# A two-layer hybrid encoder step: the heads' sums of squares as two rounded products each, and shorter norm fillers

## The chip, the cores and the metric

One Trainium2 chip, one of its cores. The metric is the device time in microseconds (us) of one execution of the whole program; lower is better.

## The reference, cut to what matters

T = 320 tokens (256 of a prompt, 64 of a running stream) of 1024 features go through two layers. Each layer is a mixer (a combined input projection, a short convolution beside a gated linear attention of 4 heads, an output projection), a layer norm, a feed-forward block (dense in layer 0, top 2 of 8 experts in layer 1) and a second layer norm. All data is float32. The change lies in the norm of the heads' outputs:

```python
o, new_s = _gla_chunked(qh, kh, vh, ah, gla_s)          # o: (B, T, 4 heads, 128)
o = o * lax.rsqrt(jnp.mean(jnp.square(o), axis=-1, keepdims=True) + LN_EPS) * gla_norm_g
y_gla = o.reshape(B, T, GLA_DV) * jax.nn.silu(g)
out = jnp.concatenate([y_conv, y_gla], axis=-1) @ w_out
```

## The kernel before, in words

Features lie on the 128 partitions and the 320 tokens along the free dimension, so a head's output is one tile of 128x320 and the sum over a head's 128 values is a sum over partitions. TensorE does it: a product with a 128x128 matrix of ones puts the sum on every partition.

Large products are made from rounded operands. A weight unit (1 MB, 128x2048) is loaded into `raw` (a ring of 6), ScalarE rounds it into `whi` (ring of 3, L1144), VectorE writes the rest into `wlo` (L1462), and TensorE adds three products of fast rounded operands (hi*hi, hi*lo, lo*hi; L664 to L666). An ordinary float32 product takes TensorE more passes; the trace shows it as two matmul records. The ones product L841 is of that kind.

All engines' programs are written out by hand, in order, with semaphores between them; there is no planner. In a mixer, TensorE works through 12 units of the input projection (24 rounded products for each of two output tiles, 48 in all) and 4 units of the output projection. On each engine `hooks` says what stands behind unit u. What matters here, per layer:

- Behind unit 8, TensorE computes the heads' outputs (`outputs`). VectorE copies them to `og` (`read_o`, L1656) and then does half of the convolution (`conv_tiles(0)`, L1700 to L1709). ScalarE squares them (`squares`, L1261) into `proj`.
- VectorE's unit 9: the rest of unit 11 (L1462), then `conv_tiles(1)`. VectorE's unit 10: the rest of unit 12 (the first of the output projection, L1462), then `weigh_o` (L1664, L1668), `rest_y` (L1731), `conv_out(0)` (L1720), `rest_y`. Its unit 11: `conv_out(1)` (L1720, waits until ScalarE has copied out the last projection tile), `rest_y`, the rest of unit 13 (L1462), and then the rest of unit 14 and the first residual tile.
- Behind unit 9 TensorE does the sums of squares (`mean_squares`, L841), then goes on with units 10 and 11. ScalarE turns the sums into 1/rms (`rms`) and afterwards rounds unit 12.
- ScalarE's unit 10 ends in rounding six of the eight tiles of y (L1282), each behind VectorE; its unit 11 copies the last two projection tiles (L1299), rounds unit 13 (L1144), and rounds the last two tiles of y.
- Output projection: TensorE waits for each rest tile of y in its first unit, and for the rest of unit 13 at its second. VectorE adds each product to the residual (L1761), ScalarE squares that (L1181) and only then rounds the next unit, whose rest VectorE takes next.
- `norm` (L725 on): the sums for the layer norm, then up to the next block TensorE has 7 filler matmuls (L744) behind norm 0 (after mixer 0) and norm 1 (after the dense block), none behind norm 2. The first product of the next block waits for `xl`, which VectorE writes (L1551).

The tile `y_split` lies in the memory of `proj`: its tiles 0 to 3 and 4 to 7 are free of other data at this point. `kg` (two tiles) is last read by the scores, before `outputs`.

Of the kernel before, what the change touches and what calls it, by code (L numbers as in the profile page):

```python
# [17 lines left out]
F32 = mybir.dt.float32  # L18
F32R = mybir.dt.float32r
I32 = mybir.dt.int32  # L20
ALU = mybir.AluOpType
ACT = mybir.ActivationFunctionType
AXX = mybir.AxisListType.X

P = 128
# [8 lines left out]
def hybrid_stream_step(nc, x_prompt, x_sample, cache_conv, state_gla, ln_mix_g, ln_mix_b, w_in, w_alpha2,  # L34
# [5 lines left out]
    T = SEQ + DEC  # L40
    _, _, HEADS, DK, DV = state_gla.shape
# [3 lines left out]
    E = moe_router.shape[2]  # L45
# [4 lines left out]
    TT = -(-T // P)  # L50
# [19 lines left out]
    TQ, TK, TV, TG = 0, 2, 4, 8  # L70
# [51 lines left out]
    with ctx:  # L122
        def sb(name, shape, dt=F32):
            return ctx.enter_context(nc.sbuf_tensor(name, shape, dt))

        def sem(name):
            return ctx.enter_context(nc.semaphore(name))
# [5 lines left out]
        x = sb("x", [P, KT, T])  # L133
        ident = sb("ident", [P, P])
        mean_d = sb("mean_d", [P, P])
        ones = sb("ones", [P, P])
        before = sb("before", [P, P])
        slot_no = sb("slot_no", [P, P])
        lower_e = sb("lower_e", [P, E, E])
# [6 lines left out]
        w_split = sb("w_split", [P, DEPTH * KT * LRC + P - LRC], F32R)  # L146
# [30 lines left out]
        def sbm(name, shape, dt=F32):  # L177
            return mix.enter_context(nc.sbuf_tensor(name, shape, dt))

        proj = sbm("proj", [P, 24, T])  # L180
# [3 lines left out]
        og = sbm("og", [P, HEADS, T])  # L184
        gb = og[:, 0:PAIRS, :]
        gc = og[:, PAIRS:2 * PAIRS, :]
        kg = sbm("kg", [P, PAIRS, T])
# [19 lines left out]
        y_split = over_proj.enter_context(nc.sbuf_tensor("y_split", [P, 16, T], F32R))  # L207
# [19 lines left out]
        def sbx(stack, name, shape, dt=F32):  # L227
# [79 lines left out]
        ps = [ctx.enter_context(nc.psum_tensor(f"ps{b}", [P, 512], F32)) for b in range(8)]  # L307
# [21 lines left out]
        by_layer = lambda name: [sem(f"{name}{l}") for l in range(DEPTH)]  # L329
# [1 line left out]
            "proj_ready", "lr_done", "lr_ready", "z_done", "gate_act", "gate_dve"))  # L331
        kd_turned, v_turned, kd_read, v_read, score_done, score_read = (by_layer(n) for n in (
            "kd_turned", "v_turned", "kd_read", "v_read", "score_done", "score_read"))
        ds_done, st_step, o_done, o_read, o_sq, ms_done, ms_act, og_step = (by_layer(n) for n in (
            "ds_done", "st_step", "o_done", "o_read", "o_sq", "ms_done", "ms_act", "og_step"))
        silu_done, cv_step, y_conv, rows_ready, rows_turned, rowsT_ready, yh_ready, yl_ready, r_ready = (
            by_layer(n) for n in ("silu_done", "cv_step", "y_conv", "rows_ready", "rows_turned", "rowsT_ready",
                                  "yh_ready", "yl_ready", "r_ready"))
# [48 lines left out]
        BUSY = {"x lands": 5, "x tile": 2, "first unit": 1, "norm": 4, "router norm": 15, "logits": 3, "first gather": 5}  # L387
# [135 lines left out]
        def _(pool):  # L523
            done = 0

            def const(ins):

                nonlocal done
                done += 1
                ins.then_inc(const_step, 1)  # L530
                pool.wait_ge(const_step, done)
# [3 lines left out]
                                     pattern=[[-1, P]], channel_multiplier=1))  # L535
            const(pool.memset(mean_d[:], 1.0 / D))
            const(pool.memset(w_wide[:, KT * E:], 0.0))
            const(pool.memset(ones[:], 1.0))
            const(pool.memset(cst[:, 0:1], LN_EPS))
            const(pool.memset(cst[:, 1:2], 1.0))  # L540
            const(pool.memset(keep[:], 1.0))
            const(pool.memset(keep[:].rearrange("p (c t) -> p c t", t=CHUNK)[:, :, 0:1], 0.0))

            const(pool.affine_select(out=before[:], in_=ones[:], compare_op=ALU.is_gt, fill=0.0, base=0,
                                     pattern=[[1, P]], channel_multiplier=-1))
            const(pool.memset(lower_e[:], 1.0))
            const(pool.affine_select(out=lower_e[:], in_=lower_e[:], compare_op=ALU.is_gt, fill=0.0, base=0,
# [28 lines left out]
            for l in range(DEPTH):  # L576

                pool.wait_ge(rowsT_ready[l], 1)
                n = (CONV_W - 1) * CT
# [7 lines left out]
                if l == 0:  # L587
# [6 lines left out]
                    fill = STATIC * P  # L594
# [65 lines left out]
        def _(pe):  # L660
# [32 lines left out]
            def keep_busy(n, bank=ps[7]):  # L693

                for _ in range(n):
                    pe.matmul(bank[:, 0:P], mean_d[:], mean_d[:], start=True, stop=True)
# [4 lines left out]
            def turn_x(k, t):  # L701
                return pe.transpose(ps[X_BANK[k]][:, P * t:P * t + TOK[t]], x_in[0:TOK[t], t, P * k:P * k + P],
                                    ident[0:TOK[t], 0:TOK[t]])

            for h in range(2):
                for t in range(TT):
                    keep_busy(BUSY["x tile"], ps[1])
                    pe.wait_ge(x_landed[h][t], 16)
                    for k in range(KT // 2 * h, min(KT // 2 * h + KT // 2, X_EARLY)):
                        mm = turn_x(k, t)  # L710
                        if t == TT - 1:
                            mm.then_inc(x_turned, 1)
            for k in range(X_EARLY, KT):
                pe.wait_ge(x_ready, k - X_EARLY + 1)
                for t in range(TT):
                    mm = turn_x(k, t)
# [8 lines left out]
            def norm(stage, wait_last):  # L725

                idle = ps[0 if stage == 3 else 7]
                pe.wait_ge(summed, (KT - 1) * (stage + 1))
                pe.matmul(ps[4][:, 0:T], mean_d[:], rstd[:], start=True, stop=False)
                wait_last()  # L730
                pe.matmul(ps[4][:, 0:T], mean_d[:], x[:, KT - 1, :], start=False, stop=True).then_inc(mean_done, 1)
                pe.wait_ge(squared, KT * (stage + 1))
                pe.matmul(ps[5][:, 0:T], mean_d[:], sq[:, (KT - 1) % 3, :], start=True, stop=False)
                pe.wait_ge(sq_summed, (KT - 1) * (stage + 1))
                pe.matmul(ps[5][:, 0:T], mean_d[:], sq_sum, start=False, stop=True).then_inc(msq_done, 1)
                if stage in PE_NORMS:
                    pe.wait_ge(mean_copied, stage + 1)
                    for k in range(OWN, KT):
                        pe.matmul(ps[C_BANK[k]][:, 0:T], ident[:], x[:, k, :], start=True, stop=False)
                        pe.matmul(ps[C_BANK[k]][:, 0:T], ident[:], neg_mean_x, start=False, stop=True  # L740
                                  ).then_inc(turned_in, 1)
                    if stage < 2:
                        for m in (96, P, 64, P, 32, P, 96):
                            pe.matmul(idle[0:m, :], w_split[:, 0:m], w_split[:, 0:512], start=True, stop=True)  # L744

            def mixer(l):
                def gates():
# [90 lines left out]
                def mean_squares():  # L838
                    for h in range(HEADS):
                        pe.wait_ge(o_sq[l], h + 1)  # L840
                        pe.matmul(ps[4 + h][:, 0:T], ones[:], proj[:, h, :], start=True, stop=True  # L841
                                  ).then_inc(ms_done[l], 1)

                hooks = {1: gates, 5: turn_kv, 6: scores, 7: states, 8: outputs, 9: mean_squares}
# [18 lines left out]
                for u in range(1, 12):  # L863
                    n = U_IN[l] + u
# [3 lines left out]
                    for half in range(2):  # L868
# [6 lines left out]
                        mm = split_product(ps[(2 * u + half) % 4][:, 0:T], tiles[KT // 2:], False, True)  # L875
# [6 lines left out]
                for u in range(UNITS_OUT):  # L882
                    n = U_OUT[l] + u
# [4 lines left out]
                    for half in range(2):  # L888
                        m = 2 * u + half
                        if m >= 4:  # L890
                            pe.wait_ge(r_ready[l], m - 3)
                        mm = split_product(ps[m % 4][:, 0:T], by_tile(n, KT, half, y_hi, y_lo), True, True)
# [60 lines left out]
            def router():  # L953
                for k in range(KT):
                    pe.wait_ge(x_ready, 3 * KT + k + 1)
                    mm = pe.matmul(ps[0][:, 0:T], w_wide[:, E * k:E * k + P], x[:, k, :], start=k == 0, stop=k == KT - 1)
                mm.then_inc(lg_done, 1)
                for j in XT_ORDER[:2]:
                    turn_rows(j)

                pe.wait_ge(rt_step, RT_LOGITS)
                for t in range(TT):
                    mm = pe.transpose(ps[1][0:TOK[t], E * t:E * t + E], lgT[:, P * t:P * t + TOK[t]], ident[0:E, 0:E])
                mm.then_inc(lg_turned, 1)
                for j in XT_ORDER[2:]:
                    turn_rows(j)
                keep_busy(BUSY["logits"], ps[0])

                pe.wait_ge(rt_step, RT_SEL)
                sel_by = lambda a, b: sel[:, a:b, :].rearrange("p t e -> p (t e)")  # L970
                pe.matmul(ps[1][:, 0:E * TT], before[:], sel_by(0, TT), start=True, stop=False)
                for t in range(1, TT):
                    pe.matmul(ps[1][:, E * t:E * TT], ones[:], sel_by(0, TT - t), start=False, stop=t == TT - 1)
                for t in range(TT):
                    mm = pe.matmul(ps[1][:, E * TT:E * TT + E], ones[:], sel_by(t, t + 1), start=t == 0, stop=t == TT - 1)
                mm.then_inc(pos_done, 1)

                keep_busy(BUSY["first gather"], ps[0])
                pe.wait_ge(cleared, 5)
                pe.wait_ge(pick_ready, 1)  # L980
                for g in range(GATHERS):
                    pe.wait_ge(xtl_ready, TT if g < 2 else 2 * TT)
                    if g < 2:
                        pe.wait_ge(acc_ready, g + 1)
                    if g >= 2:
                        pe.wait_ge(job_read, g - 1)
                    gather(g, ps[6 + g % 2])
# [149 lines left out]
        def _(act):  # L1137
# [71 lines left out]
            def mixer(l):  # L1209
# [45 lines left out]
                def squares():  # L1255
                    act.preload_act_table_set(LOG_EXP)

                    act.wait_ge(o_done[l], HEADS)
                    for h in range(HEADS):
                        act.wait_ge(o_read[l], h + 1)  # L1260
                        act.activation(proj[:, h, :], og[:, h, :], ACT.Square).then_inc(o_sq[l], 1)  # L1261

                def rms():

# [23 lines left out]
                for u in range(12):  # L1288
                    n = U_IN[l] + u
# [167 lines left out]
        def _(dve):  # L1457
# [116 lines left out]
            def mixer(l):  # L1574
# [78 lines left out]
                def read_o():  # L1653
                    for h in range(HEADS):
                        dve.wait_ge(o_done[l], h + 1)
                        dve.tensor_copy(og[:, h, :], ps[4 + h][:, 0:T]).then_inc(o_read[l], 1)  # L1656

                def weigh_o():

# [90 lines left out]
                for u in range(UNITS_OUT):  # L1750
                    n = U_OUT[l] + u
                    rest_unit(n + AHEAD)
                    for half in range(2):
                        m = 2 * u + half
# [410 lines left out]
```

## Time and profile before

| | us |
|---|---|
| median of 3 runs | 1575.9 |
| lowest, highest | 1575.33, 1576.31 |
| the profiled execution's own time | 1575.52 |
| its span in the trace | 1574.0 |
| TensorE (PE) busy | 1558.3 |
| VectorE (DVE) busy | 1238.9 |
| ScalarE (ACT) busy | 1021.7 |
| GpSimd (POOL) busy | 62.4 |

The span leaves out 1.5 us of the execution's time. A matmul's record covers its way through the array, so records overlap: the distance between two starts is what a product costs, not the length of its record. The granted clock of TensorE was 0.999 of full speed over the span. In timelines the first two columns are the start and the length in us; a bracket at the end is the engine's idle time before the instruction and what ended it.

### The profile page before, as it was taken

How to read it: one execution, taken by the hardware profiler on the slowest of the kernel's cores; microseconds unless marked ns; L12 is line 12 of the kernel's file. 1: busy time of each engine (PE TensorE's matmuls, PEld its weight loads, DVE VectorE, ACT ScalarE, POOL GpSimd, SP SyncE). 2: the span in 40 equal slices, each digit the busy share in tenths (PEclk: the TensorE clock that was granted, in tenths of full speed). 3: DMA queues.
4: the chain of work that ended last, by engine and by line, in shares of the span. 5: the costliest groups of instructions: out<-in, count | busy, mean ns of one | idle time of the engine just before them, and what ended most of it. 6: DMA issues, size and time to landing. Idle time of an engine off the chain costs nothing.

```text
span 1574.0 us, 23366 instructions
## 1 busy us (share of the span) xinstructions
PE 1558.3 (99%) x8489; PEld 1375.7 (87%) x8489; DVE 1238.9 (79%) x1414; ACT 1021.7 (65%) x1182; POOL 62.4 (4%) x97
## 2 busy tenths in 40 slices
PE   9999999999999999999999999999999999999997
PEld 8999999999999998888788888888888888888886
DVE  5577545445475688999899988989998999998996
ACT  4454333333354457778678878778878778777885
POOL 1002100000020010000200000000000001000100
PEclk9999999999999999999999999999999999999999
DMA  9524954444434344999999999999999999999992
GB/s 280 196 81 141 369 192 135 158 136 157 154 114 135 108 141 159 374 369 383 397 395 394 393 376 379 395 390 371 379 373 376 395 392 387 387 395 384 391 393 98
DMA packets 229902, 457.44 MB, mean 291 GB/s; under 512 B 10930, under 2 KB 73088, under 8 KB 229760
## 3 DMA queue, kind: packets, MB, share of 16 engines
q1 hardware_dynamic: 224288, 434.16, 76.2%
q0 software_dynamic: 5520, 22.04, 3.6%
q8 instruction: 57, 0.93, 0.2%
q14 instruction: 37, 0.30, 0.1%
HBM read 441.74 MB, written 17.58 MB: 292 GB/s over the span
## 4 chain that ended last, share of the span: by engine, by line
PE 93%; DVE 3%; DMA 1%; issue 1%; ACT 1%; SPq 0%; DVEq 0%; ACTq 0%
PE ps L1045 18%; PE ps L1020 12%; PE ps L1022 12%; PE ps L1021 12%; PE ps L664 11%; PE ps L665 11%; PE ps L666 11%; DVE wlo L1467 2%; PE ps L1058 1%; DMA raw<-in_moe_w_down 1%; DMA proj<-in_x_prompt 0%; PE ps L1094 0%; PE ps L826 0%; PE ps L1071 0%; PE ps L995 0%
## 5 line engine op out<-in xcount | busy, mean ns | idle before, releaser
L1467 DVE TENSOR_TENSOR wlo<-raw,whi 128x1024 fp32r<-128x1024 f32 x672 | 779.2, 1220 | 47.2 <-ACT whi L1148 45.7
L1148 ACT ACTIVATE whi<-raw 128x1024 fp32r<-128x1024 f32 x672 | 675.6, 1055 | 67.1 <-PE ps L1045 42.8
L1020 PE MATMUL ps<-whi,xg 128*128 128x512 f32 x896 | 354.1, 395 | 1.3 <-DVE wlo L1467 1.3
L1022 PE MATMUL ps<-whi,xg 128*128 128x512 f32 x896 | 349.5, 390 | 0.0
L1021 PE MATMUL ps<-wlo,xg 128*128 128x512 f32 x896 | 349.0, 389 | 0.0
L1462 DVE TENSOR_TENSOR wlo<-raw,whi 128x2048 fp32r<-128x2048 f32 x72 | 165.2, 2295 | 127.7 <-ACT whi L1144 127.7
L664 PE MATMUL ps<-xh,whi 128*128 128x320 f32 x832 | 259.4, 312 | 0.0
L666 PE MATMUL ps<-xh,wlo 128*128 128x320 f32 x832 | 257.1, 309 | 0.0
L665 PE MATMUL ps<-xl,whi 128*128 128x320 f32 x832 | 257.0, 309 | 0.0
L1022 PEld LDWEIGHTS ps<-whi,xg 128*128 128x128 f32 x896 | 168.2, 188 | 35.9
L1020 PEld LDWEIGHTS ps<-whi,xg 128*128 128x128 f32 x896 | 168.3, 188 | 35.3 <-issue 1.4
L1021 PEld LDWEIGHTS ps<-wlo,xg 128*128 128x128 f32 x896 | 168.4, 188 | 33.6
L1144 ACT ACTIVATE whi<-raw 128x2048 fp32r<-128x2048 f32 x72 | 137.3, 1906 | 62.5 <-PE ps L666 56.1
L664 PEld LDWEIGHTS ps<-xh,whi 128*128 128x128 f32 x832 | 156.2, 188 | 3.1 <-issue 1.4
L665 PEld LDWEIGHTS ps<-xl,whi 128*128 128x128 f32 x832 | 156.2, 188 | 0.2
L666 PEld LDWEIGHTS ps<-xh,wlo 128*128 128x128 f32 x832 | 156.2, 188 | 0.0
L1045 PE MATMUL ps<-whi,hT_hi 128*128 128x512 f32 x440 | 136.5, 391 | 0.8 <-DVE wlo L1467 0.8
L1045 PE MATMUL ps<-wlo,hT_hi 128*128 128x512 f32 x440 | 135.6, 389 | 0.0
L1045 PE MATMUL ps<-whi,hT_lo 128*128 128x512 f32 x440 | 135.5, 389 | 0.0
L1045 PEld LDWEIGHTS ps<-whi,hT_lo 128*128 128x128 f32 x440 | 82.6, 188 | 17.4
L1045 PEld LDWEIGHTS ps<-wlo,hT_hi 128*128 128x128 f32 x440 | 82.6, 188 | 17.3
L1045 PEld LDWEIGHTS ps<-whi,hT_hi 128*128 128x128 f32 x440 | 81.8, 188 | 17.5 <-issue 1.1
(351 smaller groups left out, 1420.1 us busy)
## 6 DMA issues: line engine op xcount, KB each, us to landing
raw<-in_moe_w_gate SPq DMA_DIRECT2D x112, 1024.0 KB, 8.5
raw<-in_moe_w_up SPq DMA_DIRECT2D x112, 1024.0 KB, 8.9
raw<-in_moe_w_down SPq DMA_DIRECT2D x112, 1024.0 KB, 7.8
raw<-in_w_in SPq DMA_DIRECT2D x23, 1024.0 KB, 7.5
raw<-in_ffn_w_gate SPq DMA_DIRECT2D x14, 1024.0 KB, 5.0
raw<-in_ffn_w_up SPq DMA_DIRECT2D x14, 1024.0 KB, 5.0
raw<-in_ffn_w_down SPq DMA_DIRECT2D x14, 1024.0 KB, 5.1
raw<-in_w_out SPq DMA_DIRECT2D x8, 1024.0 KB, 5.2
```

Of the source, the lines that this page charges most:

```text
L664: pe.matmul(out, wh, hi, start=start and j == 0, stop=False)
L665: pe.matmul(out, wh, lo, start=False, stop=False)
L666: mm = pe.matmul(out, wl, hi, start=False, stop=stop and j == len(pairs) - 1)
L1020: pe.matmul(bank[:], xh_k, wh, start=k == 0, stop=False)
L1021: pe.matmul(bank[:], xh_k, wl, start=False, stop=False)
L1022: mm = pe.matmul(bank[:], xl_k, wh, start=False, stop=k == KT - 1)
L1045: mm = pe.matmul(ps[4 + d][:], hT[:, c % 2, k, :], slot(w, n, SPLIT, 2)[:, j, 512 * d:512 * d + 512], start=fc == 0 and k == 0 and hT is h ...
L1058: mm = pe.transpose(bank[:, P * f:P * f + P], hm[:, c % 2, P * f:P * f + P], ident[:])
L1144: act.activation(flat(whi, n, SPLIT), flat(raw, n, RAW), ACT.Copy).then_inc(hi_ready, 2)
L1148: act.activation(part(whi, n, SPLIT, h), part(raw, n, RAW, h), ACT.Copy).then_inc(hi_ready, 1)
L1462: dve.tensor_tensor(flat(wlo, n, SPLIT), flat(raw, n, RAW), flat(whi, n, SPLIT).bitcast(F32), ALU.subtract).then_inc(lo_ready, 2)
L1467: dve.tensor_tensor(part(wlo, n, SPLIT, h), part(raw, n, RAW, h), part(whi, n, SPLIT, h).bitcast(F32), ALU.subtract).then_inc(lo_ready, 1)
```

## The change

- The matrix of ones becomes a tile of the rounded type (`ones_r`); its float32 view serves all other uses.
- ScalarE's squares are written rounded, into `y_split` tiles 0 to 3.
- VectorE, directly behind the four copies of `read_o` and ahead of `conv_tiles(0)`, gets 8 operations of 128x320: for each head the square once more, unrounded, into one of the two tiles of `kg`, and the difference from the rounded square into `y_split` tiles 4 to 7.
- TensorE's 4 float32 products (L841) become 8 rounded ones, hi and lo of each head added in PSUM; the second waits for VectorE.
- The 7 fillers behind norms 0 and 1 (rounded operands, 512 columns) become `keep_busy(4)`: 4 float32 products of `mean_d` with 128 columns.

```diff
-        ones = sb("ones", [P, P])
+        ones_r = sb("ones_r", [P, P], F32R)
+        ones = ones_r[:, :].bitcast(F32)
...
-                    if stage < 2:
-                        for m in (96, P, 64, P, 32, P, 96):
-                            pe.matmul(idle[0:m, :], w_split[:, 0:m], w_split[:, 0:512], start=True, stop=True)
+                    keep_busy(BUSY["norm"] if stage < 2 else 0, idle)
...
                         pe.wait_ge(o_sq[l], h + 1)
-                        pe.matmul(ps[4 + h][:, 0:T], ones[:], proj[:, h, :], start=True, stop=True
+                        pe.matmul(ps[4 + h][:, 0:T], ones_r[:], y_split[:, h, :], start=True, stop=False)
+                        pe.wait_ge(o_sq_lo, 2 * (HEADS * l + h) + 2)
+                        pe.matmul(ps[4 + h][:, 0:T], ones_r[:], y_split[:, TV + h, :], start=False, stop=True
                                   ).then_inc(ms_done[l], 1)
...
-                        act.wait_ge(o_read[l], h + 1)
-                        act.activation(proj[:, h, :], og[:, h, :], ACT.Square).then_inc(o_sq[l], 1)
+                        act.wait_ge(o_read, HEADS * l + h + 1)
+                        act.activation(y_split[:, h, :], og[:, h, :], ACT.Square).then_inc(o_sq[l], 1)
...
                         dve.wait_ge(o_done[l], h + 1)
-                        dve.tensor_copy(og[:, h, :], ps[4 + h][:, 0:T]).then_inc(o_read[l], 1)
+                        dve.tensor_copy(og[:, h, :], ps[4 + h][:, 0:T]).then_inc(o_read, 1)
+                    for h in range(HEADS):
+                        dve.wait_ge(o_read, HEADS * l + h + 1)
+                        dve.tensor_tensor(kg[:, h % 2, :], og[:, h, :], og[:, h, :], ALU.mult).then_inc(o_sq_lo, 1)
+                        dve.wait_ge(o_sq[l], h + 1)
+                        dve.wait_ge(o_sq_lo, 2 * (HEADS * l + h) + 1)
+                        dve.tensor_tensor(y_split[:, TV + h, :], kg[:, h % 2, :], y_split[:, h, :].bitcast(F32),
+                                          ALU.subtract).then_inc(o_sq_lo, 1)
```

## Rows read from the trace of the kernel before

**Rows 1.** Page, part 1: busy us, share of the span, instructions of each engine
```profile
PE 1558.3 (99%) x8489; PEld 1375.7 (87%) x8489; DVE 1238.9 (79%) x1414; ACT 1021.7 (65%) x1182; POOL 62.4 (4%) x97
```
**Rows 2.** Page, part 4: the chain that ended last, by engine
```profile
PE 93%; DVE 3%; DMA 1%; issue 1%; ACT 1%; SPq 0%; DVEq 0%; ACTq 0%
```
**Rows 3.** Timeline, layer 0, TensorE around the sums of squares
```profile
97.25 0.31 PE L666 MATMUL ps<-xh,wlo 128*128 128x320 f32 x1
97.40 2.31 PE L841 MATMUL ps<-proj,ones 128*128 128x320 f32 x8
...
99.70 0.31 PE L665 MATMUL ps<-xl,whi 128*128 128x320 f32 x1
```
**Rows 4.** Timeline, layer 0, VectorE from the heads' outputs to unit 13
```profile
91.74 0.42 DVE L1700 TENSOR_TENSOR u_mem<-proj 128x256 f32<-128x256 f32 x1
...
95.89 2.29 DVE L1462 TENSOR_TENSOR wlo<-raw,whi 128x2048 fp32r<-128x2048 f32 x1
...
103.62 2.29 DVE L1462 TENSOR_TENSOR wlo<-raw,whi 128x2048 fp32r<-128x2048 f32 x1 [1.30 <-ACT whi L1144]
105.83 0.55 DVE L1664 SCALAR_TENSOR_TENSOR og<-og,prm,proj 128x320 f32<-128x320 f32 x1
106.41 0.49 DVE L1668 TENSOR_TENSOR og<-og,proj 128x320 f32<-128x320 f32 x1
106.82 0.54 DVE L1664 SCALAR_TENSOR_TENSOR og<-og,prm,proj 128x320 f32<-128x320 f32 x1
...
114.37 0.42 DVE L1720 TENSOR_TENSOR proj<-proj,v_tok 128x256 f32<-128x256 f32 x1 [0.91 <-ACT proj L1299]
...
117.27 2.28 DVE L1462 TENSOR_TENSOR wlo<-raw,whi 128x2048 fp32r<-128x2048 f32 x1
```
**Rows 5.** Timeline, layer 0, ScalarE at the last projection tiles
```profile
112.83 0.42 ACT L1299 ACTIVATE proj<-ps 128x320 f32<-128x320 f32 x1
113.83 0.44 ACT L1299 ACTIVATE proj<-ps 128x320 f32<-128x320 f32 x1 [0.57 <-PE ps L666]
114.16 1.91 ACT L1144 ACTIVATE whi<-raw 128x2048 fp32r<-128x2048 f32 x1
```
**Rows 6.** Timeline, layer 0, TensorE: output units 12, 13, and its last product
```profile
113.63 0.31 PE L664 MATMUL ps<-y_split,whi 128*128 128x320 f32 x1
...
120.67 0.31 PE L664 MATMUL ps<-y_split,whi 128*128 128x320 f32 x1
...
141.64 0.31 PE L666 MATMUL ps<-y_split,wlo 128*128 128x320 f32 x1
```
**Rows 7.** Timeline, layer 0, VectorE: residual tiles 1, 3 and 7 of the output projection
```profile
122.58 0.48 DVE L1761 SCALAR_TENSOR_TENSOR x<-x,ps 128x320 f32<-128x320 f32 x1
...
129.01 0.48 DVE L1761 SCALAR_TENSOR_TENSOR x<-x,ps 128x320 f32<-128x320 f32 x1
...
141.99 0.49 DVE L1761 SCALAR_TENSOR_TENSOR x<-x,ps 128x320 f32<-128x320 f32 x1
```
**Rows 8.** Timeline, layer 1, VectorE: rest of unit 13, residual tiles 5 and 7
```profile
557.06 2.29 DVE L1462 TENSOR_TENSOR wlo<-raw,whi 128x2048 fp32r<-128x2048 f32 x1
...
574.74 0.49 DVE L1761 SCALAR_TENSOR_TENSOR x<-x,ps 128x320 f32<-128x320 f32 x1 [0.28 <-PE ps L666]
...
581.78 0.49 DVE L1761 SCALAR_TENSOR_TENSOR x<-x,ps 128x320 f32<-128x320 f32 x1 [1.38 <-PE ps L666]
```
**Rows 9.** Timeline, layer 1, TensorE: first product of output unit 13
```profile
560.46 0.31 PE L664 MATMUL ps<-y_split,whi 128*128 128x320 f32 x1
```
**Rows 10.** Timeline, norm 0: fillers, first and third rest tile
```profile
147.24 2.03 PE L744 MATMUL ps<-w_split 128*96 128x512 f32 x7
...
148.09 0.55 DVE L1551 SCALAR_TENSOR_TENSOR xl<-x,prm,xh 128x320 fp32r<-128x320 f32 x1
...
151.02 0.19 PEld L664 LDWEIGHTS ps<-xh,whi 128*128 128x128 f32 x1 [0.25 <-DVE xl L1551]
```
**Rows 11.** Windows near the end: length, busy us by engine, granted clock, DMA
```profile
1568.00:1570.00 2.00, 0.00 (x0) 0.00 (x0) 2.00 (x4) 0.50 (x2) 0.00 (x0) 0.93 0.70 262
```

More of the change, by code:

```diff
@@ L333, in hybrid_stream_step @@
             "kd_turned", "v_turned", "kd_read", "v_read", "score_done", "score_read"))
-        ds_done, st_step, o_done, o_read, o_sq, ms_done, ms_act, og_step = (by_layer(n) for n in (
-            "ds_done", "st_step", "o_done", "o_read", "o_sq", "ms_done", "ms_act", "og_step"))
+        ds_done, st_step, o_done, o_sq, ms_done, ms_act, og_step = (by_layer(n) for n in (
+            "ds_done", "st_step", "o_done", "o_sq", "ms_done", "ms_act", "og_step"))
+        o_read, o_sq_lo = sem("o_read"), sem("o_sq_lo")
         silu_done, cv_step, y_conv, rows_ready, rows_turned, rowsT_ready, yh_ready, yl_ready, r_ready = (
@@ L537, in _ @@
             const(pool.memset(w_wide[:, KT * E:], 0.0))
-            const(pool.memset(ones[:], 1.0))
+            const(pool.memset(ones, 1.0))
             const(pool.memset(cst[:, 0:1], LN_EPS))
@@ L542, in _ @@
             const(pool.memset(keep[:].rearrange("p (c t) -> p c t", t=CHUNK)[:, :, 0:1], 0.0))
-            const(pool.affine_select(out=before[:], in_=ones[:], compare_op=ALU.is_gt, fill=0.0, base=0,
+            const(pool.affine_select(out=before[:], in_=ones, compare_op=ALU.is_gt, fill=0.0, base=0,
                                      pattern=[[1, P]], channel_multiplier=-1))
@@ L972, in router @@
                 for t in range(1, TT):
-                    pe.matmul(ps[1][:, E * t:E * TT], ones[:], sel_by(0, TT - t), start=False, stop=t == TT - 1)
+                    pe.matmul(ps[1][:, E * t:E * TT], ones, sel_by(0, TT - t), start=False, stop=t == TT - 1)
                 for t in range(TT):
-                    mm = pe.matmul(ps[1][:, E * TT:E * TT + E], ones[:], sel_by(t, t + 1), start=t == 0, stop=t == TT - 1)
+                    mm = pe.matmul(ps[1][:, E * TT:E * TT + E], ones, sel_by(t, t + 1), start=t == 0, stop=t == TT - 1)
                 mm.then_inc(pos_done, 1)
```

## The prediction

> **What bounds the kernel now.** I read the busy times first: TensorE is busy for 1558.3 of 1574.0 us, VectorE for 79% [rows 1]. The chain that ended last says the same: 93% of it is TensorE, 3% VectorE [rows 2]. So a microsecond taken from TensorE's stream is a microsecond gained, but only where no other engine is next in line. The 3% of VectorE warn of places where it is, so I then read the timelines of the mixer, engine by engine. The reader is to see two clocks there. TensorE's: an output unit of 48 products takes 120.67 - 113.63 = 7.04 us, 0.147 us a product [rows 6]. VectorE's: from one residual tile to its counterpart a unit later it needs 6.43 us (122.58 to 129.01), and two such steps further it would be at 141.87; the row says 141.99 [rows 7], 0.12 us late, because TensorE's last product only started at 141.64 [rows 6]. VectorE enters the output projection late, makes up 0.6 us a unit, and has just caught up when the norm begins. There is nothing left for it to lose there.
>
> **TensorE's part: the gain.** The eight records L841 of a layer occupy the stream from 97.40 to 99.55 (the product at 99.70 is the second behind them, so one distance of 0.147 earlier) [rows 3], 2.15 us. Eight rounded products of 320 columns at 0.147 take 1.17 us. Saved: 0.98 us a layer, 1.96 us in both. That the new ones run at 0.147 is taken from L664 to L666, same shape and type. The new second product of each head waits for VectorE's rest. VectorE is at this point at 91.74 [rows 4], and even with the dearest price below it is done by 96.5, 0.9 us before TensorE arrives at 97.40: that wait costs nothing.
>
> **VectorE's part: the price.** Per layer 4 squares and 4 differences of 128x320 go in at 91.74, ahead of the convolution. The nearest rows are L1664 and L1668 [rows 4]. A tensor-tensor operation lasts 0.49 us; the next one that doesn't depend on it starts 0.41 us after it (106.41 to 106.82); one that waits for its predecessor's result starts 0.03 us after that one's end (105.83 + 0.55 to 106.41). So a head costs 0.49 + 0.03 + 0.41 = 0.93 us and the block 3.72 us. Bounds: 8 x 0.41 = 3.3 us if nothing waited, and 8 x 0.58 = 4.6 us if each operation cost what the dependent pair shows from start to start. I take 3.72, as the code alternates just like L1664 and L1668. The differences wait for ScalarE's squares too, but these are made at the pace of the copies and are ahead.
>
> The Trainium skill, "VectorE: DVE Perf Modes", section "The DRAIN you can't avoid", says that the next operation does not start until the pipe is empty, and that a semaphore costs nothing on top. By that the block would be 8 x 0.49 = 3.9 us and the sum below 0.4 us larger. The rows disagree: 106.82 lies 0.08 us before the end of the operation started at 106.41.
>
> **Where the 3.72 us go.** I follow them down VectorE's program in layer 0.
> - The rest of unit 11 moves from 95.89 to 99.6 and ends at 101.9 [rows 4]. TensorE needs it 7.04 us before 113.63, at 106.6, or 105.6 with its gain [rows 6]. Hidden.
> - Ahead of the rest of unit 12 VectorE had 1.30 us idle, waiting for ScalarE; with the 0.08 by which an operation may start before its predecessor's end 1.38 us are absorbed. Left: 2.34 us.
> - `weigh_o` and everything on y moves by 2.34. ScalarE follows, as it rounds y tile by tile. Its copy of the tile before the last moves from 112.83 to 115.17, the last one follows 0.33 later (113.83 to 114.16 is that distance) at 115.50, where it was at 113.83 and had waited 0.57 for TensorE [rows 5]. Left: 1.67 us.
> - VectorE's own wait there (0.91, at 114.37) gives nothing more, as it waits for that very copy. The rest of unit 13 goes from 117.27 to 118.94 and ends at 121.22 [rows 4].
> - TensorE, 0.98 early, would start unit 13 at 119.69. It gets its rest at 121.22, and 0.10 later starts (114.27 to 114.37 is that distance from one engine's end to another's start [rows 4, 5]): 121.32 in place of 120.67, 0.65 late. The gain is gone here, a new wait stands in its place.
> - It does not end there. VectorE and ScalarE enter the output projection 1.67 us later than before, and their own period of 6.43 us is no shorter. Residual tiles 1 and 3 come at 124.25 and 130.68, tile 7 at 141.87 + 1.67 = 143.54 where it was at 141.99: 1.55 us late. TensorE is only 0.65 late by then, and idles for 0.9 us before the norm's last sum. Everything after this is a chain through the norm. Layer 0: +1.55 us.
>
> Layer 1 has the same program and the same waits, except in its output projection. There VectorE already waits for TensorE before residual tiles 5 and 7, 0.28 and 1.38 us [rows 8], so its lag of 1.67 is swallowed down to what TensorE itself is late. That is again the rest of unit 13: 557.06 + 2.29 + 1.67 + 0.10 = 561.12 against 560.46 [rows 8, 9]. Layer 1: +0.66 us.
>
> **The fillers.** The seven start at 147.24 and end their stream about when the first rest tile is written: it is started at 148.09 and done at 148.64. Four short ones end earlier and may let the first product start up to 0.2 us sooner. That is worth nothing: at the third tile (151.02) TensorE waits for VectorE's `xl` by 0.25 us [rows 10], and goes on doing so, so VectorE's pace sets that stretch. Bounds: a gain of 0.2 us at each of the two places, a loss only through the clock (below). I take 0. The rounded type of the ones matrix and the semaphores cost nothing; the DMA queue SP is moved only in that loads wait for rests up to 3.7 us later, with six units of lead. The expert stage is TensorE's (rows 1 and 2), so what the mixers lose is not made up there.
>
> **Sum.** 1.55 + 0.66 + 0 = +2.2 us on the profiled execution's 1575.52 (span 1574.0, 1.5 around it): 1577.7. The median of the runs shown, 1575.9, is 0.4 above that execution, so I forecast 1578.1, 0.14% slower. A measurement of this kernel can tell about 0.2%, 3.15 us, from no change, so this counts as the same.
>
> **Rivals.**
> - *The block is dearer, and the change is slower by over 0.2%.* Beyond the absorbed parts each microsecond of the block arrives twice, once a layer: total = 2 x block - 5.2. At 4.64 us a block, where each of the 8 operations takes the 0.58 of the dependent pair, it is +4.1 us: 1580.0. It passes +3.15 at a block of 4.2 us. For it: every operation of the block touches what its neighbour or ScalarE has just written, and the differences wait on two semaphores. Against: 0.41 behind L1668, which has waits behind it too.
> - *VectorE's work is hidden, TensorE's gain stands*: -1.96 and up to -0.4 from the fillers: 1573.7. For it: VectorE is idle 21% of the time, with gaps of 1.30 and 0.91 in this very stretch. Against: both gaps end with ScalarE, which itself follows VectorE or TensorE, and only 2.05 us are swallowed.
> - *The lag vanishes before the norm in layer 0 as well* (if ScalarE's rounding, not VectorE, sets the 6.43): then both layers lose 0.66, +1.3: 1577.2. Against: the lag of 1.67 sits in both engines.
> - *The clock falls behind the shorter fillers.* They leave TensorE idle some 0.6 us ahead of the next block. In a stretch of 2 us without any matmul near the end, the granted clock was still 0.93 on the mean, and only then went to half (2.4 to 1.2 GHz) [rows 11]. If it fell, a product of the first unit would take twice 0.147, up to 7 us at each of two places: 1585 or more.
>  The Trainium skill, "TensorE: Matmul & The Clock Gate", section "HAM oscillation — how this bites in real kernels", warns that idle gaps let the gate fall and make the next products cold. That would be this rival's time; the rows 11 don't bear it out for a gap this short.
> - *The change doesn't do what it says*: the rounded ones product might run at the float32 pace, then nothing is saved on TensorE. As VectorE sets both layers' ends, that would change little: unit 13 starts at 121.3 either way.
>
> **Chances.** Forecast 0.52 (0.12 of it beyond +3.15, as an error of 0.5 us in a block would do it), dearer block 0.20, hidden 0.12, lag vanishes early 0.10, clock 0.03, something else 0.03. Over 0.2% faster would need more than the whole saving of TensorE: 0.05. Slower: 0.12 + 0.17 of the dearer block + 0.03 of the clock = 0.32. The same: 0.63. The range takes in the hidden case nearly and the dearer block: 1574.2 to 1580.6. The forecast's own range is 1576.8 to 1579.6.
>
> **What would show it.** Right: TensorE's sums of squares take 1.2 us a layer without a wait; 8 operations in 3.7 us on VectorE; a wait of TensorE for `wlo` of 1 us or more at the second output unit in both mixers, in part already at y's last two rest tiles; residual tile 7 of layer 0 right behind VectorE's own work, with TensorE idle 0.9 us; in layer 1 none there; the wait at the third tile behind the norms unchanged; clock 1.00 throughout. Wrong: no idle time of TensorE ahead of unit 13; a block of over 4.2 us or under 3.3; a granted clock below 1 behind a norm; or a changed expert stage, which nothing here touches.

## The result, and the profile after

The changed kernel takes 1578.8 us (median of 20 runs, 1577.94 to 1580.28) against 1575.64 for the kernel before, measured beside it (20 runs, 1574.93 to 1576.81). The ratio is 1.0018 with a 95% interval of 1.0012 to 1.0025: 2.8 us slower by the ratio (the two medians lie 3.16 apart). That is within the 0.2% that the prediction counts as the same, but the interval leaves out no change at all: it is a small loss. The forecast was 1578.1, or +2.2 us.

The page, parts 1 and 4, of the changed kernel:

```profile
span 1577.3 us, 23394 instructions
...
PE 1557.9 (99%) x8491; PEld 1375.5 (87%) x8491; DVE 1245.6 (79%) x1430; ACT 1020.4 (65%) x1182; POOL 62.6 (4%) x97
...
PE 87%; DVE 7%; issue 2%; ACT 2%; DMA 1%; SPq 0%; DVEq 0%; ACTq 0%
```

TensorE is as busy as before (1557.9 against 1558.3 us [rows 1]), VectorE 6.7 us busier. The chain that ended last says where the time went: TensorE's share fell from 93% to 87%, VectorE's rose from 3% to 7% [rows 2]. The busy times alone would not tell it.

TensorE at the sums of squares, layer 0, where [rows 3] had eight records of 0.27 us distance:

```profile
97.46 0.31 PE L668 MATMUL ps<-xh,wlo 128*128 128x320 f32 x1
97.61 0.31 PE L841 MATMUL ps<-y_split,ones_r 128*128 128x320 f32 x1
97.75 0.31 PE L843 MATMUL ps<-y_split,ones_r 128*128 128x320 f32 x1
...
98.64 0.31 PE L843 MATMUL ps<-y_split,ones_r 128*128 128x320 f32 x1
98.78 0.31 PE L666 MATMUL ps<-xh,whi 128*128 128x320 f32 x1
```

97.61 to 98.78 is 1.17 us for the eight, no wait among them: the gain of 0.98 us a layer is there. (All of this trace lies 0.21 us later than the one before when it comes to the heads' outputs, which is the chance of the start.) VectorE, layer 0, beside [rows 4]:

```profile
91.95 0.48 DVE L1661 TENSOR_TENSOR kg<-og 128x320 f32<-128x320 f32 x1
92.53 0.49 DVE L1664 TENSOR_TENSOR y_split<-kg,y_split 128x320 fp32r<-128x320 f32 x1
92.94 0.48 DVE L1661 TENSOR_TENSOR kg<-og 128x320 f32<-128x320 f32 x1
...
95.94 0.42 DVE L1709 TENSOR_TENSOR u_mem<-proj 128x256 f32<-128x256 f32 x1
...
106.43 2.29 DVE L1464 TENSOR_TENSOR wlo<-raw,whi 128x2048 fp32r<-128x2048 f32 x1
...
116.48 0.43 DVE L1729 TENSOR_TENSOR proj<-proj,v_tok 128x256 f32<-128x256 f32 x1 [0.23 <-ACT proj L1301]
...
119.38 2.28 DVE L1464 TENSOR_TENSOR wlo<-raw,whi 128x2048 fp32r<-128x2048 f32 x1
...
143.96 0.48 DVE L1770 SCALAR_TENSOR_TENSOR x<-x,ps 128x320 f32<-128x320 f32 x1
```

The block takes 95.94 - 91.95 = 3.99 us. The idle 1.30 before the rest of unit 12 is gone (106.43, no bracket), the wait for ScalarE's copy has shrunk from 0.91 to 0.23. TensorE's weight loads (PEld; the bracket is the idle time before them) show new waits for one of the last rest tiles of y and at unit 13, in layer 0; a shorter one, for the first rest tile of y at the first product of unit 12, shows in its products (PE):

```profile
113.22 0.39 PE L666 MATMUL ps<-y_split,whi 128*128 128x320 f32 x1 [0.19 <-DVE y_split L1740]
```
```profile
119.11 0.19 PEld L666 LDWEIGHTS ps<-y_split,whi 128*128 128x128 f32 x1 [0.65 <-DVE y_split L1740]
121.72 0.19 PEld L666 LDWEIGHTS ps<-y_split,whi 128*128 128x128 f32 x1 [0.84 <-DVE wlo L1464]
```

Behind the last residual tile, TensorE and then VectorE's first centering of norm 0:

```profile
142.79 0.31 PE L668 MATMUL ps<-y_split,wlo 128*128 128x320 f32 x1
...
143.69 0.81 PE L731 MATMUL ps<-rstd,mean_d 128*128 128x320 f32 x2 [0.48 <-DVE rstd L1519]
```
```profile
146.23 0.89 DVE L1535 TENSOR_TENSOR x<-x,kd_tok 128x320 f32<-128x320 f32 x2 [1.26 <-ACT kd_tok L1188]
```

The kernel before has 0.91 in that last bracket (its centering starts at 143.91). The copy of ScalarE that both wait for, in the changed kernel and in the kernel before:

```profile
145.34 0.44 ACT L1188 ACTIVATE kd_tok<-ps 128x320 f32<-128x320 f32 x1 [0.23 <-PE ps L733]
```
```profile
143.38 0.44 ACT L1186 ACTIVATE kd_tok<-ps 128x320 f32<-128x320 f32 x1 [0.24 <-PE ps L731]
```

It ended at 145.34 + 0.44 = 145.78, so VectorE started 0.45 us behind it; before it was 0.09 (143.38 + 0.44 to 143.91). Nothing in the working had this, and the experiments follow it up. The chain that ended last names the stretch in the changed kernel: VectorE's queue (DVEq) is past its wait at 145.81 + 0.02, and then comes "issue", time in which the engine waits for nothing that the profile shows:

```profile
145.81 0.02 DVEq L1537
145.83 0.40 issue
```

For all runs I measured two distances in the trace that no chance of the start can move. N0: from VectorE's first copy of layer 0's heads' outputs to the first rest tile of norm 0. N2: from the same copy in layer 1 to the first centering of norm 2. The stretch between the two is 381.8 us in every one of them (before: 148.09 to 529.93; changed: 150.51 to 532.36), and what follows N2 takes 990.3 and 990.2 us in these two. So N0 and N2 hold the whole difference. Each is read from one trace of a kernel, but the four kernels with the whole block at its place (changed, e1, e2, e6) agree to 0.03 us, whereas the part behind N2 takes 989.7 to 992.1 us over all traces with no order by kernel. That is why the distances can tell apart what the measured times can't.

| kernel | N0, us | N2, us | sum against before | measured ratio (95%) |
|---|---|---|---|---|
| before | 57.95 | 53.78 | | |
| changed | 60.16 | 54.72 | +3.15 | 1.0018 (1.0012 to 1.0025) |
| e1 changed again | 60.17 | 54.71 | +3.15 | 1.0019 (1.001 to 1.0028) |
| e2 VectorE's block alone | 60.15 | 54.73 | +3.15 | 1.0024 (1.0015 to 1.0034) |
| e3 TensorE's part alone | 56.98 | 52.80 | -1.95 | 0.9988 (0.9979 to 0.9997) |
| e4 convolution first | 57.42 | 52.80 | -1.51 | 0.9989 (0.998 to 0.9998) |
| e5 fillers alone | 57.96 | 53.78 | +0.01 | 1.0 (0.9991 to 1.0009) |
| e6 changed, old fillers | 60.18 | 54.73 | +3.18 | 1.002 (1.0011 to 1.0029) |
| e7 squares together | 59.39 | 53.95 | +1.61 | 1.001 (1.0001 to 1.0019) |
| e8 before, 12 instructions more | 58.40 | 53.78 | +0.45 | one run |
| e9 before, convolution first | 57.96 | 53.78 | +0.01 | 0.9999 (0.999 to 1.0008) |
| e10 e4, shifted | 56.98 | 52.80 | -1.95 | 0.999 (0.9981 to 0.9999) |
| e11 e4 and e7 | 57.43 | 52.80 | -1.50 | 0.9991 (0.9982 to 1.0) |

### The profile page after: what moved, and what is told of

Its sections match the earlier page's. It is cut to its first block, busy times and chain, and to the rows that moved or that the text cites. A ratio compares the mean times of both kernels' runs of the same rounds, so it can differ in the third digit from the quotient of the medians.

```text
span 1577.3 us, 23394 instructions
## 1 busy us (share of the span) xinstructions
PE 1557.9 (99%) x8491; PEld 1375.5 (87%) x8491; DVE 1245.6 (79%) x1430; ACT 1020.4 (65%) x1182; POOL 62.6 (4%) x97
## 4 chain that ended last, share of the span: by engine, by line
PE 87%; DVE 7%; issue 2%; ACT 2%; DMA 1%; SPq 0%; DVEq 0%; ACTq 0%
PE ps L1047 18%; PE ps L1022 12%; PE ps L1024 12%; PE ps L1023 12%; PE ps L666 9%; PE ps L668 9%; PE ps L667 9%; DVE wlo L1469 2%; PE ps L1060 1%; DMA raw<-in_moe_w_down 1%; DVE wlo L1464 1%; ACT whi L1146 1%; DMA proj<-in_x_prompt 0%; PE ps L1096 0%; DVE x L1567 0%
```

## The experiments

**e1, the changed kernel again.**

> The changed kernel once more, on the chip of the experiments. Every theory expects the ratio on record, about 1.002 (+2.8 us). The profile of the changed kernel showed one thing the working lacks: behind residual tile 7 of layer 0, VectorE's first centering starts 0.45 us after ScalarE's end in place of 0.09. If this belongs to the kernel it is there again; if it is the chance of one execution, it is 0.1 here.

1578.62 us against 1575.81. Its trace has the late centering again (bracket 1.26). It belongs to the kernel, not to one execution.

**e2, VectorE's block alone.** The kernel before, with

```diff
+                    for h in range(HEADS):
+                        dve.wait_ge(o_read, HEADS * l + h + 1)
+                        dve.tensor_tensor(kg[:, h % 2, :], og[:, h, :], og[:, h, :], ALU.mult).then_inc(o_sq_lo, 1)
+                        dve.wait_ge(o_sq[l], h + 1)
+                        dve.wait_ge(o_sq_lo, 2 * (HEADS * l + h) + 1)
+                        dve.tensor_tensor(y_split[:, TV + h, :], kg[:, h % 2, :], proj[:, h, :],
+                                          ALU.subtract).then_inc(o_sq_lo, 1)
```

(ScalarE's `rms` also gets a wait for the differences; they are written 1 us or more before it, so it holds nothing up.)

> The kernel before with VectorE's 8 operations a layer added at the place where the change has them, but with the float32 ones products kept (the differences are written and not used) and the old fillers. Theory: TensorE's gain of 0.98 us a layer reaches neither end, VectorE's lag sets both; so this is as slow as the whole change: +2.8 us over the kernel before (residual tile 7 of layer 0 at +1.8, TensorE's second output unit of layer 1 at +0.9). Rival, that gain and price simply add (TensorE -1.96, VectorE the rest): +4.8 us.

1579.42 us, ratio 1.0024; N0 and N2 as in the whole change. The 1.96 us that TensorE's new products save make no difference once the block is there: price and gain don't add, VectorE's lateness sets both ends. TensorE's stream, with its old sums of squares, shows one wait only, that for the rest of unit 13:

```profile
121.23 0.19 PEld L665 LDWEIGHTS ps<-y_split,whi 128*128 128x128 f32 x1 [0.84 <-DVE wlo L1464]
```

The interval of the ratio alone would still admit the rival (+4.8 us is 1.0030); the distances, +3.15, don't.

**e3, TensorE's part alone.** The changed kernel without VectorE's operations, and

```diff
-                        pe.wait_ge(o_sq_lo, 2 * (HEADS * l + h) + 2)
-                        pe.matmul(ps[4 + h][:, 0:T], ones_r[:], y_split[:, TV + h, :], start=False, stop=True
+                        pe.matmul(ps[4 + h][:, 0:T], ones_r[:], y_split[:, h, :], start=False, stop=True
```

> The changed kernel without VectorE's 8 operations, old fillers; the second product of each head reads the rounded square once more (so the sums are twice the right ones and the rests are left out). Theory: with VectorE's lag away the whole of TensorE's gain arrives, -1.96 us against the kernel before, 1573.7 us: residual tile 7 of layer 0 about 0.9 us earlier and the second output unit of layer 1 0.98 earlier. Rival, that layer 0's VectorE and ScalarE loop has nothing to give (it was only 0.12 us ahead): -1.1 us.

1573.45 us against 1575.81, ratio 0.9988. N0 is 0.97 and N2 0.98 shorter: the gain of 0.98 arrives in both layers. Layer 0 had that to give although VectorE was only 0.12 us ahead there [rows 6, 7], since with earlier sums ScalarE rounds unit 12 earlier and VectorE itself moves up (residual tile 7 at 140.86, 50.87 behind the copy; 51.85 before). That was in the theory and not in the rival.

**e4, the convolution first.** The changed kernel with

```diff
-                         6: [mask_scores], 7: [state_chain], 8: [read_o, conv_tiles(0)], 9: [conv_tiles(1)],
+                         6: [mask_scores], 7: [state_chain], 8: [conv_tiles(0), read_o], 9: [conv_tiles(1)],
```

> The changed kernel with one line turned round on VectorE: the first half of the convolution (4.15 us) stands ahead of the copies of the heads' outputs, where VectorE was idle for 6.03 us, in place of behind the 8 operations. Theory: the lag is absorbed whole, TensorE's gain of 0.98 us a layer arrives: -1.95 us against the kernel before, about 1573.7. No wait of TensorE at the second output unit. Rival, that VectorE is slower than ScalarE's and TensorE's needs for another reason than the place of the block: still slower than before, +1 us or more.

1574.44 us against 1575.81, ratio 0.9989. In VectorE's timeline the convolution now fills the idle time; of 6.03 us before the copies 1.89 are left:

```profile
87.01 1.14 DVE L1718 SCALAR_TENSOR_TENSOR kd_tok<-u_mem,prm,kd_tok 128x322 f32<-128x322 f32 x2
90.04 1.68 DVE L1658 COPY og<-ps 128x320 f32<-128x320 f32 x4 [1.89 <-PE ps L833]
91.64 0.48 DVE L1661 TENSOR_TENSOR kg<-og 128x320 f32<-128x320 f32 x1
...
95.63 2.28 DVE L1464 TENSOR_TENSOR wlo<-raw,whi 128x2048 fp32r<-128x2048 f32 x1
```

The block still takes 3.99 us of VectorE, and costs nothing. So it is its place that made the change slower (at the old place its length counts too, see e7). N2 is 0.98 shorter than before, N0 only 0.53: the 0.45 missing are the late centering, which is here too.

**e5 and e6, the fillers.** The kernel before with the new ones, and the changed kernel with the old ones:

```diff
-                    if stage < 2:
-                        for m in (96, P, 64, P, 32, P, 96):
-                            pe.matmul(idle[0:m, :], w_split[:, 0:m], w_split[:, 0:512], start=True, stop=True)
+                    keep_busy(BUSY["norm"] if stage < 2 else 0, idle)
```

> The kernel before with nothing but the shorter fillers behind norms 0 and 1. Theory: no difference, 1575.8 us within 0.5; TensorE idles some 0.6 us before the first product and waits for VectorE's third rest tile at the same time as before; granted clock 1.00. Rivals: 0.2 us gained at each place (-0.4), or the clock falls (+7 or more).

> The changed kernel with the old fillers: what the fillers are worth beside the rest of the change. Theory: as the changed kernel, +2.8 us over the kernel before. Rival, that they matter here: off that by 0.4 or more.

e5: 1575.9 against 1575.87; e6: 1578.92, like e1. TensorE around norm 0 in e5 (compare [rows 10]), and the granted clock there:

```profile
146.90 1.05 PE L696 MATMUL ps<-mean_d 128*128 128x128 f32 x8
148.20 0.39 PE L664 MATMUL ps<-xh,whi 128*128 128x320 f32 x1 [0.25 <-DVE xl L1549]
...
150.43 0.41 PE L664 MATMUL ps<-xh,whi 128*128 128x320 f32 x1 [0.23 <-DVE xl L1549]
```
```profile
147.00:149.00 2.00, 1.75 (x14) 1.59 (x13) 2.00 (x6) 1.64 (x4) 0.85 (x1) 1.00 0.04 12
```

The first product waits now, the third tile waits as before, 2.92 us behind the start of the first rest tile at 147.51 (2.93 in [rows 10]). The granted clock in this stretch is 1.00, the upper of its two levels (2.4 GHz). Norm 1 lies in the 381.8 us between N0 and N2, which are the same here, so nothing is gained or lost there either.

**e7, the squares together.**

```diff
+                    squares_of = [kg[:, 0, :], kg[:, 1, :], ga[:, 0, :], ga[:, 1, :]]
+                    for h in range(HEADS):
+                        dve.wait_ge(o_read, HEADS * l + h + 1)
+                        dve.tensor_tensor(squares_of[h], og[:, h, :], og[:, h, :], ALU.mult).then_inc(o_sq_lo, 1)
                     for h in range(HEADS):
...
```

> The changed kernel with VectorE's 8 operations in another order: the four squares first (into four free tiles), then the four differences, so that none waits for its predecessor. Theory: each operation starts 0.41 us behind the last, the block shrinks from 3.99 to 3.3 us a layer, and as every microsecond of the block arrives twice, the kernel gets 1.4 us faster than the changed one: +1.4 over the kernel before. In layer 1 no less, as TensorE waits for the rest of unit 13 there too. Rival, that the lag is set by ScalarE: no gain against the changed kernel.

```profile
91.65 0.88 DVE L1662 TENSOR_TENSOR kg<-og 128x320 f32<-128x320 f32 x2
92.45 0.89 DVE L1662 TENSOR_TENSOR ga<-og 128x320 f32<-128x320 f32 x2
93.25 0.89 DVE L1666 TENSOR_TENSOR y_split<-kg,y_split 128x320 fp32r<-128x320 f32 x2
94.06 0.89 DVE L1666 TENSOR_TENSOR y_split<-ga,y_split 128x320 fp32r<-128x320 f32 x2
94.86 0.42 DVE L1711 TENSOR_TENSOR u_mem<-proj 128x256 f32<-128x256 f32 x1
```

The block takes 3.21 us, 0.78 less, and N0 and N2 are each 0.77 shorter than in the changed kernel: a microsecond of the block arrives once a layer, one to one. 1577.23 us, ratio 1.001, where e1 had 1.0019. So the lag begins with VectorE's block; the rival, that ScalarE sets it, is out.

**e8, twelve instructions more.** The kernel before, with this behind the states of layer 0:

```diff
+                    if l == 0:
+                        for i in range(12):
+                            dve.memset(rstd[:, i:i + 1], 0.0)
```

> The kernel before with 12 one-column memsets on VectorE in layer 0 alone, in the 6.03 us in which it waits for the heads' outputs. They are as many instructions as the change adds there (8 operations and 4 more waits) and cost no time where they stand. All three kernels with the 8 operations (the changed one, the block alone, the convolution first) show VectorE's first centering of norm 0 start 0.45 us after ScalarE's end, and the two without show 0.09. Theory: it depends on where the instruction lies in VectorE's program, and appears here too (rest tiles of norm 0 some 0.35 us later than in the kernel before). Rival: it comes from the work that the 8 operations do or displace; then it is 0.09 here.

VectorE's memsets, and its first centering of norm 0; ScalarE's copy that it waits for:

```profile
80.67 0.21 DVE L1654 MEMSET rstd<- 128x1 f32 x12
...
143.90 0.89 DVE L1533 TENSOR_TENSOR x<-x,kd_tok 128x320 f32<-128x320 f32 x2 [1.26 <-ACT kd_tok L1186]
```
```profile
143.01 0.44 ACT L1186 ACTIVATE kd_tok<-ps 128x320 f32<-128x320 f32 x1 [0.24 <-PE ps L731]
```

The memsets ran at 80.67, ahead of the rest of an earlier unit for which VectorE waits, and not in the 6.03 us directly ahead of the copies as I had written; they cost nothing there either. The copies of the heads' outputs come no later for the memsets (6.03 us idle before them, as before), residual tile 7 is at its old distance (51.85), and yet the centering starts 143.90 - 143.45 = 0.45 us behind ScalarE, and N0 is 0.45 us longer. The rival (the work of the block) is out: 12 instructions that have nothing to do with the block bring the same stall. (It is one trace; its one measured time, 1577.01, can't tell 0.45 us.)

**e9, the turned order in the kernel before.**

> The kernel before with nothing but the turned order (first half of the convolution ahead of the copies of the heads' outputs). It tells whether the gain of the changed kernel with that order is TensorE's or the order's own. Theory: in the kernel before the rest of unit 12 waits for ScalarE (1.30 us idle), so an earlier VectorE changes nothing: 1575.8, no difference within 0.3 us. Rival: the order itself is worth the 1 to 2 us.

1575.49 against 1575.53, N0 and N2 unchanged. The rest of unit 11 came 1.65 us earlier (94.24), that of unit 12 at 103.62 as ever, behind ScalarE. The order is worth nothing by itself, and what e4 gains is TensorE's.

**e10, the same shift as in e8 on top of e4.**

> The changed kernel with the convolution first, and 12 more one-column memsets on VectorE in layer 0, in the time in which it waits for the heads' outputs: VectorE's program behind them lies 24 instructions later than in the kernel before. Theory (a stall that belongs to a place in VectorE's program): the 0.45 us between ScalarE's end and the first centering of norm 0 are 0.09 again, the rest tiles of norm 0 come 0.4 us earlier after the last residual tile, and the kernel is 0.4 us faster than with the convolution first alone, about 1574.0. Rival: every shift stalls it, no difference.

```profile
142.81 0.89 DVE L1535 TENSOR_TENSOR x<-x,kd_tok 128x320 f32<-128x320 f32 x2 [0.91 <-ACT kd_tok L1188]
143.62 0.48 DVE L1542 SCALAR_TENSOR_TENSOR u_mem<-u_mem,ps 128x320 f32<-128x320 f32 x1
144.14 0.33 DVE L1545 TENSOR_SCALAR u_mem<-u_mem 128x320 f32<-128x320 f32 x1
```

The chain that ended last has, between VectorE's wait and the centering,

```profile
142.75 0.02 DVEq L1537
142.77 0.04 issue
```

where the changed kernel has 0.40. In the trace the stall is gone (0.91), and N0 is 56.98, as in e3: 0.44 less than in e4. The measured times can't tell so little: 1574.1 against 1575.53 here, 1574.44 against 1575.81 there. By the distances the whole gain of 1.95 us is there.

**e11, both orders.**

> The changed kernel with the convolution first and the four squares ahead of the four differences. Theory: with the convolution first VectorE has room, so a block shorter by 0.7 us changes nothing: as the convolution first alone, -1.4 to -1.7 us against the kernel before, 1574.3. Rival, that the block still sets the end: 0.7 or 1.4 us faster still.

1573.99 against 1575.53, ratio 0.9991 (0.9982 to 1.0). N0 and N2 as in e4: a shorter block has no price left to take away. (The interval reaches 1.0, so this run's times alone would not show a gain.)

e3 leaves part of the sum out; of the kernels that compute all of it, e4, e10 and e11 are ahead of both others: by 1.4 to 1.5 us of the kernel before, and e4 by 4.2 us of the changed kernel on the same chip (e1).

## Why the prediction was right

- *What bounds it.* Right in its mechanism: VectorE enters the output projection later and, in layer 0, the period that it shares with ScalarE keeps the lag to the end (residual tiles 1, 3, 5, 7 at 124.69, 131.11, 137.53, 143.96, always 6.42 to 6.43 apart; in each lap VectorE still waits 1.48 to 1.65 us for ScalarE's rounding, which itself waits for VectorE's residual tile, so neither engine sets the period alone). The share of the chain moved as it had to.
- *TensorE's gain*, 0.98 us a layer and no wait for the rests of the squares: as forecast, to the hundredth. e3 shows that it would arrive.
- *VectorE's price*: mis-sized. 3.72 us were forecast, 3.99 measured. The difference of each head starts 0.58 behind its square, which I had as 0.49 + 0.03 = 0.52, since L1668 starts 0.03 behind the end of L1664 [rows 4]. The pair that I took as the model repeats every 0.99 us from start to start (105.83 to 106.82 [rows 4]), 3.96 for four; taking 0.06 a head off it, because a square is shorter than L1664, was the step that failed. Against that pair these have a second semaphore to wait for and a shorter predecessor. Neither explains the 0.10 by itself: the kernel before has a pair with both, L1517, which waits on two semaphores, behind L1761 of 0.48 us, and it starts 0.52 behind it:

```profile
122.58 0.48 DVE L1761 SCALAR_TENSOR_TENSOR x<-x,ps 128x320 f32<-128x320 f32 x1
123.10 0.49 DVE L1517 TENSOR_TENSOR rstd<-rstd,x 128x320 f32<-128x320 f32 x1
```

  What makes the 0.10 stays open. By the rule of the Trainium skill ("VectorE: DVE Perf Modes", "The DRAIN you can't avoid") the prediction's estimate was 3.9 us, near the measured block. The trace does not bear out its reason: in e7, where none waits for the one before, operations of 0.48 us start 0.40 us apart. The same section also says that an operation that isn't held starts earlier, which the prediction left out; e7 agrees with that.
- *Where the block goes*: absorbed before unit 12 (106.43 - 103.62 - 0.21 = 2.60 of the 3.99 are left, 1.39 absorbed, 1.38 forecast) and at ScalarE's copy, as worked out. The rest of unit 13 comes 119.38 - 117.27 - 0.21 = 1.90 us late (1.67 forecast), residual tile 7 of layer 0 143.96 - 141.99 - 0.21 = 1.76 (1.55), layer 1's end 0.94 (0.66). TensorE's last output product is 142.79 - 141.64 - 0.21 = 0.94 late, so it idles for the remaining 0.82 ahead of the norm's last sum (0.9 forecast). The wait for unit 13 was to be 1 us or more; it is 0.84, as part of the lateness is already taken at two rest tiles of y, the first of them ahead of unit 12, where I had no wait.
- *What the working lacked*: 0.45 us in norm 0. 0.36 of it pass before the first centering, 0.10 at L1545 (0.43 us long in place of 0.33). e8 makes it in the kernel before by 12 instructions that cost nothing where they stand, e10 takes it away with 12 more. Forecast 2.21, measured 3.15 in the trace: 0.21 more in layer 0 and 0.28 more in layer 1, nearly all of it the block's 0.27, and 0.45 of this. Put into the prediction's own rule, 2 x block - 5.2, the measured block gives 2.8; the trace without the stall has 2.70. The misses all point the same way, so the forecast is not near by errors that cancel.
- *The fillers*: 0, as forecast (e5, e6).
- *The rivals*: "hidden" and "the lag vanishes in layer 0" did not happen; "dearer block" named the term that was too small, at a price (4.64) that was too high. "The ones product at float32 pace" was refuted on TensorE, and e2 shows that it would have changed nothing, as said. The clock did not fall: 0.998 over the changed kernel's span, 0.999 before, and 1.00 behind norm 0 in e5.

## What to carry to other kernels

When work moves from the busiest engine to one with idle time, the share of idle time says nothing; look for where in its program the new work is put, and which unit of the busiest engine waits for what stands behind it. Here the same 8 operations made the kernel 2.7 us slower with the convolution behind them (e2, without the stall) and cost nothing with it ahead of them (e10 is as fast as e3), and that one line of order decided between slower and faster than before. Helpers whose lap (6.43 us here) is only a little shorter than the busiest engine's (7.04) carry a delay on for a whole stage: compare the two periods before pricing a delay at its first wait.

## What the runs showed of the hardware

VectorE can lose 0.36 us (0.45 with the next operation's 0.10) at one place of its program, depending on how many instructions lie ahead of it: none with the kernel before's, 0.45 with 12 more (e1, e2, e4, e6, e7, e8, e11), none with 24 more (e10). Counted in the traces, waits included, the first centering of norm 0 is VectorE's 180th instruction in the kernel before, e3, e5 and e9, the 192nd in every kernel with the stall, and the 204th in e10. The centering of norm 2 has 0.91 in its bracket in every trace, so it is not a matter of the centering as such.

The traces also list DMA packets of the kind "instruction". One on queue q14 lies near this place and moves with VectorE's program alone. The queue's line in narrow windows, for the kernel before (146.5 to 146.7, 2.6 us or more behind the start of the centering), the changed kernel (147.0 to 147.2, 0.8 to 1.0 behind it) and e10 (137.6 to 137.7, 5.1 or more ahead of it):

```profile
q14 instruction: 1, 0.01, 19.3%
```
```profile
q14 instruction: 1, 0.01, 10.9%
```
```profile
q14 instruction: 1, 0.01, 26.3%
```

So the stall and this packet both sit where the count of VectorE's instructions puts them. But the packet starts behind the stall and can't itself be what VectorE waits for; the cause stays open. In the timeline the stall is listed as idle time behind ScalarE's work; that work's end, worked out from its own row, or the "issue" of the chain gives it away.

A dependent pair of tensor-tensor operations of 128x320 started 0.58 us apart, an independent one 0.40 to 0.41.
